# Second even attention of a two-block kernel on one core: heads in pairs on the two row halves of TensorE, values by half heads with a zero-padded V

## The chip, the cores and the metric

The kernel runs on one core of one Trainium2 chip. The metric is the device time of one execution in microseconds; given is the median of three runs. A core has TensorE (PE, matrix products into the PSUM banks), VectorE (DVE), ScalarE (ACT), GpSimd (POOL) and a DMA queue issued by SyncE (SP). The PSUM has 8 banks of 512 fp32 columns. TensorE's array has 128 rows; an operand that lies on 64 partitions uses one half of them.

## What is computed

Two blocks follow each other on 512 tokens of width 1024. The change lies in the even mixer of the second block, which runs two attentions side by side: a global one and one with a window of 128 tokens and a sink, each with 8 query heads and 2 key and value heads of width 64.

```python
def global_gqa(q, k, v):
...
        s = jnp.einsum('bqkgd,bskd->bkgqs', qi, k, preferred_element_type=jnp.float32) * scale
        p = jax.nn.softmax(s, axis=-1).astype(v.dtype)
        return jnp.einsum('bkgqs,bskd->bqkgd', p, v)

def windowed_gqa_sink(q, k, v, sink):
...
    valid = (jnp.abs(qpos - kpos) <= WINDOW) & (kpos >= 0) & (kpos < s_len)
    s = jnp.where(valid[None, :, None, None], s, NEG_INF)
    m = jnp.maximum(jnp.max(s, axis=-1), sk)
    p = jnp.exp(s - m[..., None])
    denom = jnp.sum(p, axis=-1) + jnp.exp(sk - m)
    p = (p / denom[..., None]).astype(v.dtype)
    o = jnp.einsum('bnkgqs,bnskd->bnqkgd', p, v_slab)

def even_mixer(h, w_in, q_gain, k_gain, sink, w_out, rope1, rope_axial):
    proj = h @ w_in
...
    oa = global_gqa(qa, ka, va)
...
    ob = windowed_gqa_sink(qb, kb, vb, sink)
    return jnp.concatenate([oa, ob], axis=-1) @ w_out
```

## The kernel before

Every fp32 matrix product is done as three products of rounded parts: each operand is split into a high part and the rest, and high x high, high x low and low x high are added in one bank (`PASSES`). The high part is written by ScalarE (a copy into fp32r), the low part by VectorE (a subtraction). Weights come through SP in groups of 128 x 1024, which POOL splits the same way (`split`, L296 to L300); most matmuls are in `group` (L384), a tile of 128 features by 512 tokens from one group. Each engine has one program with a fixed order of instructions, and semaphores between them; no scheduler moves anything.

The stage in question comes behind the projection `even2` (12 groups), whose last steps normalise and rotate queries and keys on VectorE and ScalarE, and ahead of the output projection `even2_out` (8 groups). Queries lie with features on partitions: tile i holds head i on partitions 0 to 63 and head 4 + i on partitions 64 to 127, and the keys and values of the two groups lie likewise. So a score product works on 64 rows, and its rows are those of the side s.

The work is cut into 64 units: u = 0 to 31 global, u = 32 to 63 banded; a unit is one head and one block j of 128 queries. `unit_b` orders them by group g, tile i, side s and block j, so four units of one head follow each other, then four of the other side. For one unit the steps are:

- `scores_b` (PE, L705): three matmuls of 64 rows, 512 columns in the global half, 256 or 384 (two or three chunks of keys) in the banded one, into one of three banks (4, 5, 0). It waits for the exp of unit u - 3.
- DVE takes the negated maximum (L1563); in the banded half it adds the mask, writes the sum to SBUF and takes the maximum in one instruction with a read-out behind it (L1571, twice), then brings in the sink (L1575).
- ACT takes the exp with a row sum (L1123), in the banded half also the exp of the sink (L1128); DVE the reciprocal (L1585, with L1583 ahead of it in the banded half); POOL scales the row (L338).
- `turn_b` (PE, L716): 2 to 4 transposes into bank 6 or 7, three units behind the scores.
- ACT copies the high part out (L1113), DVE subtracts for the low part (L1592), into `E_PT`.
- `values_b` (PE, L736): eight units behind the scores, when a head's four units are transposed. A step is one chunk of keys, three matmuls; four steps make a head, in bank 2 or 3 in turn. The stationary side is a chunk of `E_V` with 128 columns, those of both value heads, so both halves of the output fill and only that of the head's side is used. In the banded half the four steps have 512, 256, 384 and 256 columns; the first is whole so that it sets the bank, and for it POOL zeroes a corner of `E_PT` (L332).
- At the end of a head ACT copies the 64 partitions of its side (L1135) and DVE subtracts (L1599), into `Y2`.

PE goes through them as scores of u, values step of u - 8, transposes of u - 3:

```python
for u in range(64 + 8):
    if u == 3:
        pe.wait_ge(s_qlo, 22)
    if u < 64:
        scores_b(u)
    if u >= 8:
        values_b(u - 8)
    if 3 <= u < 67:
        turn_b(u - 3)
```

DVE's order for u is maximum of u, reciprocal of u - 1, low part of u - 3, and once in four units the output of a head. ACT's is high part of u - 3, exp of u, and the output of a head.

## Time and profile before

| | us |
|---|---|
| median of 3 runs | 2723.18 (2721.81 to 2744.44) |
| span of the profiled execution | 2728.4 |
| PE busy | 2627.8 (96%) |
| DVE busy | 1199.8 (44%) |
| ACT busy | 602.6 (22%) |
| POOL busy | 1572.9 (58%) |

No separate time of the profiled execution is given besides its span; the span lies 5.2 us above the median. Busy shares are sums over the whole program; matmuls are pipelined and their ends are modelled, so a busy PE may still be waiting in part. The granted clock of TensorE stands as a share of 2.4 GHz: 0.50 is 1.2 GHz. A duration of a row with "x3" goes from the start of the first to the modelled end of the last. In a chain each piece lasts until the next one takes over, so its pieces add up to the time. Times of rows are counted from the start of the span.

### The profile page before, as it was taken

The page shows a single profiled execution, that of the slowest core. Times are in us where ns is not written, and L with a number is a line of the kernel's source. Part 1 is how long each engine was busy: PE and PEld are TensorE (multiplying, and loading weights), DVE is VectorE, ACT ScalarE, POOL GpSimd, SP SyncE. Part 2 cuts the span into 40 slices and gives each one's busy share as a digit, 9 for nine tenths or more (in the row PEclk, how much of TensorE's full clock was granted, in tenths as well). Part 3 has the DMA queues.
Part 4 walks back from the last instruction along what each step waited for, and adds up shares of the span by engine and source line. Part 5 has one row for each costly group of instructions (what it writes and reads, how often), then busy time and mean ns, then how long its engine had stood idle before and what let it go on. Part 6 is the DMA issues. An engine that isn't in the chain of part 4 may idle for free.

```text
span 2728.4 us, 32300 instructions
## 1 busy us (share of the span) xinstructions
PE 2627.8 (96%) x11402; PEld 2046.6 (75%) x11402; DVE 1199.8 (44%) x1719; ACT 602.6 (22%) x1122; POOL 1572.9 (58%) x1329
## 2 busy tenths in 40 slices
PE   7999988999999999999999999999999998999998
PEld 2876446888788886667788887888887776788886
DVE  4353656446333314657533322333213777533311
ACT  3222431112111102256211111111102344211100
POOL 2523015666666775523666776676776664666675
PEclk9999999999999999889999999999999999999999
DMA  6311432333323332100332333333332211233332
GB/s 229 126 41 60 141 121 89 100 94 98 93 92 100 100 101 76 65 1 3 101 100 93 99 102 99 95 97 95 103 102 91 74 59 40 93 100 92 100 100 85
DMA packets 69058, 249.07 MB, mean 91 GB/s; under 512 B 7664, under 2 KB 10224, under 8 KB 68336
## 3 DMA queue, kind: packets, MB, share of 16 engines
q1 hardware_dynamic: 63936, 232.81, 27.3%
q10 hardware_dynamic: 5040, 15.16, 1.6%
q8 instruction: 51, 0.84, 0.1%
q14 instruction: 31, 0.25, 0.0%
HBM read 245.85 MB, written 2.10 MB: 91 GB/s over the span
## 4 chain that ended last, share of the span: by engine, by line
PE 89%; DVE 6%; ACT 2%; issue 2%; DMA 1%; POOL 0%; SPq 0%; ACTq 0%; DVEq 0%; POOLq 0%
PE pb L384 68%; PE pb L830 3%; PE pb L776 2%; PE pb L705 2%; PE pb L736 1%; PE pb L791 1%; PE pb L443 1%; PE pb L552 1%; PE pb L815 1%; PE pb L800 1%; PE pb L716 1%; PE pb L425 1%; PE pb L482 1%; PE pb L525 1%; PE pb L592 1%
## 5 line engine op out<-in xcount | busy, mean ns | idle before, releaser
L384 PE MATMUL pb<-ar,w_hi 128*128 128x512 f32 x5600 | 1739.2, 392 | 10.5 <-DVE ar L1264 4.5
L384 PEld LDWEIGHTS pb<-ar,w_hi 128*128 128x128 f32 x5600 | 1049.5, 188 | 246.5 <-issue 15.3
L384 PE MATMUL pb<-ar,w_lo 128*128 128x512 f32 x2800 | 1091.2, 390 | 0.0
L300 POOL TENSOR_TENSOR w_lo<-raw,w_hi 128x1024 fp32r<-128x1024 f32 x396 | 990.7, 2502 | 33.0
L296 POOL TENSOR_TENSOR still<-still 128x1 f32<-128x1 f32 x396 | 80.2, 202 | 932.0 <-PE pb L384 627.1
L384 PEld LDWEIGHTS pb<-ar,w_lo 128*128 128x128 f32 x2800 | 526.8, 188 | 110.4
L297 POOL TENSOR_SCALAR w_hi<-raw 128x1024 fp32r<-128x1024 f32 x396 | 421.0, 1063 | 0.0
L1522 DVE TENSOR_TENSOR tb<-pb,nb 128x512 f32<-128x512 f32 x88 | 60.9, 692 | 417.8 <-PE pb L384 417.8
L1443 DVE SCALAR_TENSOR_TENSOR x<-pb,x 128x512 f32<-128x512 f32 x48 | 36.5, 760 | 381.9 <-PE pb L384 381.9
L1528 DVE TENSOR_TENSOR ar<-tb,ar 128x512 f32 x88 | 156.2, 1775 | 91.0 <-ACT ar L1077 91.0
L1077 ACT ACTIVATE ar<-tb 128x512 f32 x88 | 55.7, 633 | 531.5 <-DVE tb L1525 531.5
L866 ACT ACTIVATE nb<-x 128x512 f32<-128x512 f32 x72 | 44.9, 625 | 382.9 <-DVE x L1443 377.2
L1075 ACT ACTIVATE tb<-tb 128x512 f32<-128x512 f32 x88 | 55.8, 634 | 252.1 <-DVE tb L1520 252.1
L1455 DVE SCALAR_TENSOR_TENSOR ar<-x,vec,ar 128x512 fp32r<-128x512 f32 x32 | 87.4, 2731 | 25.3 <-ACT ar L1038 25.3
L1520 DVE TENSOR_TENSOR tb<-pb,nb 128x512 f32<-128x512 f32 x88 | 60.9, 692 | 85.5 <-PE pb L384 85.5
L338 POOL TENSOR_SCALAR tb<-tb,tiny 128x512 f32<-128x512 f32 (+2 forms) x64 | 39.1, 612 | 102.9 <-DVE tiny L1585 102.9
L316 POOL TENSOR_TENSOR tb<-rt 128x256 f32<-128x256 f32 (+1 forms) x64 | 56.6, 887 | 67.9 <-PE pb L800 67.9
L1525 DVE TENSOR_TENSOR tb<-tb 128x512 f32<-128x512 f32 x88 | 87.9, 998 | 11.5
L830 PE MATMUL pb<-ar,w_hi 128*128 128x512 f32 x256 | 84.1, 409 | 0.0
L1222 DVE TENSOR_TENSOR nb<-nb 128x512 f32<-128x512 f32 (+1 forms) x70 | 73.3, 1047 | 21.1 <-ACT nb L866 19.6
L1038 ACT ACTIVATE ar<-x,vec 128x512 fp32r<-128x512 f32 x32 | 23.2, 724 | 210.8 <-DVE x L1443 210.8
L705 PE MATMUL pb<-ar 64*128 64x512 f32 (+2 forms) x192 | 63.2, 444 | 1.4 <-ACT tb L1123 1.4
(196 smaller groups left out, 2394.0 us busy)
## 6 DMA issues: line engine op xcount, KB each, us to landing
raw<-wstream SPq DMA_DIRECT2D x444, 512.0 KB, 3.5
x<-xt ACTq DMA_DIRECT2D x2, 2048.0 KB, 9.1
rt<-nbias ACTq DMA_DIRECT2D x16, 192.0 KB, 2.4
tb<-dft ACTq DMA_DIRECT2D x1, 2048.0 KB, 8.6
out<-x ACTq DMA_DIRECT2D x8, 256.0 KB, 2.2
tb<-ctxt ACTq DMA_DIRECT2D x1, 1024.0 KB, 13.4
rt<-rope ACTq DMA_DIRECT2D x1, 1024.0 KB, 4.8
rt<-nmask ACTq DMA_DIRECT2D x1, 640.0 KB, 3.8
```

Source lines behind the costliest of these rows:

```text
L296: pool.tensor_tensor(still[:, 0:1], still[:, 1:2], still[:, 2:3], ALU.add)
L297: pool.tensor_scalar(w_hi[:, n % SPLIT, :], raw[:, j, :], 1.0, 1.0, ALU.mult, ALU.mult)\
L300: pool.tensor_tensor(w_lo[:, n % SPLIT, :], raw[:, j, :], w_hi[:, n % SPLIT, :].bitcast(F32), ALU.subtract).then_inc(s_split, 1)
L384: mm = pe.matmul(pb[:, bank, :], W[a][:, n % SPLIT, k * P:(k + 1) * P], rhs(b, k0 + k), start=(first and k == 0 and i == 0), stop=(last an ...
L705: mm = pe.matmul(pb[:, S_BANKS[u % 3], 0:(hi - lo) * P], E_Q[g][a][rows, i, j * P:(j + 1) * P], E_K[g][b][rows, lo * P:hi * P], start=(q = ...
L830: mm = pe.matmul(pb[:, m % 2, :], W[a][:, m % SPLIT, k * P:(k + 1) * P], H[b][:, k, :], start=(k == 0 and i == 0), stop=(k == KT - 1 and i ...
L1222: dve.tensor_tensor(acc[:, 0:n], acc[:, 0:n], sq[k % 2][:, 0:n], ALU.add)\
L1455: dve.scalar_tensor_tensor(H[1][:, m, :], x[:, m, :], vcol(gain, i + m), H[0][:, m, :].bitcast(F32), ALU.mult, ALU.subtract)\
L1520: dve.tensor_tensor(tb[:, j, :], pb[:, 2 * j, :], rstd, ALU.mult).then_inc(s_ev, 1)
L1522: dve.tensor_tensor(tb[:, 4 + j, :], pb[:, 2 * j + 1, :], rstd, ALU.mult).then_inc(s_ev, 1)
L1525: dve.tensor_tensor(tb[:, 6 + j, :], tb[:, 2 + j, :], tb[:, 4 + j, :], ALU.mult)\
L1528: dve.tensor_tensor(tile(A_FFN[1], t * 2 + j), tb[:, 6 + j, :], tile(A_FFN[0], t * 2 + j).bitcast(F32), ALU.subtract)\
```

## The change

The 64 units become 32 pairs: w = 0 to 15 global, 16 to 31 banded. A pair is the two heads of one tile i (sides 0 and 1) for one block j.

- Scores: for each of the three passes one matmul on the rows of side 0 and one on those of side 1, into two banks: (0, 1) and (4, 5) in turn. They wait for both exps of pair w - 2.
- DVE takes the maxima of both banks in one instruction of 1024 columns in the global half; in the banded half two masked maxima and one tiny instruction for both sinks (whose negation is computed once ahead of the loop). The reciprocals of both heads are one instruction, now of pair w - 1 and ahead of the maxima of pair w.
- ACT takes two exps behind each other, in the banded half then two exps of sinks; POOL scales two rows.
- Transposes two pairs behind the scores, in three banks (3, 6, 7) in turn by head.
- Values four pairs behind the scores: one head of the pair, half of its queries (two blocks, 256 columns), all its chunks of keys, 12 matmuls of 256 columns in the global half; in the banded half 6 of 256 and 3 of 128 without the empty corners, so POOL's zeroing of corners of `E_PT` goes. The stationary side `E_VP` has 128 columns of which the 64 of the other side are zero, so both heads of a tile add into one bank, 2, for all tiles.
- Output: one copy and one subtraction of 128 partitions for two heads, once in four pairs; values of the next two heads wait for it.
- In `even2` POOL zeroes the four parts of `E_VP` (1024 columns each) between weight splits, and V is copied and subtracted in two pieces (64 columns of each chunk) where there was one.

The third attention keeps its own list of steps under a new name (`WHOLE`), and counts of semaphores that follow are adapted.

```diff
-        E_V = [[area(8192 + 6144 * g + 5120 + 512 * s, 4, P) for s in range(2)] for g in range(2)]
+        E_VP = [[ar[:, o:o + 8 * P].rearrange("p (s k c) -> p s k c", s=2, k=4)
+                 for o in (8192 + 6144 * g + 5120, 20480 + 1024 * g)] for g in range(2)]
...
-        S_BANKS = (4, 5, 0)
+        S_BANKS = ((0, 1), (4, 5))
+        T_BANKS = (3, 6, 7)
...
-        P_ROWS = (0, 1, 2, 4)
+        P_ROWS = ((0, 1), (2, 4), (5, 6))
...
+                if seg == "even2":
+                    for i in range(groups):
+                        split(g0 + i, n0 + i)
+                        if 2 <= i < 6:
+                            half = E_VP[(i - 2) // 2][i % 2]
+                            pool.memset(half.rearrange("p s k c -> p (s k c)").bitcast(F32), 0.0).then_inc(s_zero, 1)
+                    continue
...
-                    for u in range(64):
-                        if u in (34, 38):
-
-                            b = (u - 34) // 4
-                            pool.wait_ge(bt["o"], 7 + b)
-                            for part in range(2):
-                                pool.tensor_scalar(E_PT[b][part][:, 1, 3 * P:4 * P], ident, 0.0, 0.0, ALU.mult,
-                                                   ALU.mult).then_inc(s_zero, 1)
...
+                    for w in range(32):
+                        n = TOK if w < 16 else P * len(chunks_of(w % 4))
+                        pool.wait_ge(bt["r"], w + 1)
+                        for side in range(2):
+                            p = tb[:, P_ROWS[w % 3][side], 0:n]
+                            pool.tensor_scalar(p, p, tiny[:, 40 + 2 * (w % 4) + side:41 + 2 * (w % 4) + side], 1.0,
+                                               ALU.mult, ALU.mult).then_inc(bt["p"], 1)
...
+            def pair_b(w):
+
+                return w // 16, (w % 16) // 4, w % 4
+
+            def scores_b(w):
+                g, i, j = pair_b(w)
+                if w >= 2:
+                    pe.wait_ge(bt["e"], 2 * (w - 2) + 2)
                 lo, hi = (0, 4) if g == 0 else (chunks_of(j)[0], chunks_of(j)[-1] + 1)
                 for q, (a, b) in enumerate(PASSES):
-                    mm = pe.matmul(pb[:, S_BANKS[u % 3], 0:(hi - lo) * P], E_Q[g][a][rows, i, j * P:(j + 1) * P],
-                                   E_K[g][b][rows, lo * P:hi * P], start=(q == 0), stop=(q == 2))
-                mm.then_inc(bt["s"], 1)
...
-            def turn_b(u):
-                g, i, s, j = unit_b(u)
-                pe.wait_ge(bt["p"], u + 1)
-                if u >= 2:
-                    pe.wait_ge(bt["lo"], u - 1)
-                n = 4 if g == 0 else len(chunks_of(j))
...
-            GLOBAL = [(k, 0, 4) for k in range(4)]
-            BANDED = [(1, 0, 4), (0, 0, 2), (2, 1, 4), (3, 2, 4)]
...
-                if c == 0:
-                    pe.wait_ge(bt["lo"], 4 * head + 4)
-                    if head >= 2:
-                        pe.wait_ge(bt["ylo"], head - 1)
-                    if g == 1:
-                        pe.wait_ge(s_zero, 2 * (head % 2) + 2)
-                k, q0, q1 = (BANDED if g else GLOBAL)[c]
-                for q, (a, b) in enumerate(PASSES):
-                    mm = pe.matmul(pb[:, 2 + head % 2, q0 * P:q1 * P], E_V[g][a][:, k, :],
-                                   E_PT[head % 2][b][:, k, q0 * P:q1 * P],
-                                   start=(c == 0 and q == 0), stop=(c == 3 and q == 2))
-                if c == 3:
+                    for side in range(2):
+                        rows = slice(64 * side, 64 * side + 64)
+                        mm = pe.matmul(pb[:, S_BANKS[w % 2][side], 0:(hi - lo) * P],
+                                       E_Q[g][a][rows, i, j * P:(j + 1) * P], E_K[g][b][rows, lo * P:hi * P],
+                                       start=(q == 0), stop=(q == 2))
+                        if q == 2:
+                            mm.then_inc(bt["s"], 1)
+
+            def turn_b(w):
+                g, i, j = pair_b(w)
+                for side in range(2):
+                    n = 2 * w + side
+                    pe.wait_ge(bt["p"], n + 1)
+                    if n >= 3:
+                        pe.wait_ge(bt["lo"], n - 2)
+                    for c in range(4 if g == 0 else len(chunks_of(j))):
+                        mm = pe.transpose(pb[:, T_BANKS[n % 3], c * P:(c + 1) * P],
+                                          tb[:, P_ROWS[w % 3][side], c * P:(c + 1) * P], ident)
+                    mm.then_inc(bt["t"], 1)
+
+
+            GLOBAL = [[(k, 2 * half, 2 * half + 2) for k in range(4)] for half in range(2)]
+            BANDED = [[(1, 0, 2), (0, 0, 2), (2, 1, 2)], [(2, 2, 4), (3, 2, 4), (1, 2, 3)]]
+
+            def values_b(half, side):
+
+                head = half // 2
+                g = head // 4
+                pe.wait_ge(bt["lo"], 4 * half + 2 + side + 1)
+                if side == 0 and half % 2 == 0 and head >= 1:
+                    pe.wait_ge(bt["ylo"], head)
+                pieces = (BANDED if g else GLOBAL)[half % 2]
+                for c, (k, q0, q1) in enumerate(pieces):
+                    for q, (a, b) in enumerate(PASSES):
+                        mm = pe.matmul(pb[:, 2, q0 * P:q1 * P], E_VP[g][a][:, side, k, :],
+                                       E_PT[side][b][:, k, q0 * P:q1 * P],
+                                       start=(side == 0 and c == 0 and q == 0),
+                                       stop=(side == 1 and c == len(pieces) - 1 and q == 2))
+                if side == 1:
                     mm.then_inc(bt["o"], 1)
...
-            pe.wait_ge(s_vlo, 4)
+            pe.wait_ge(s_vlo, 6)
...
+            for w in range(32 + 4):
+                if w == 1:
                     pe.wait_ge(s_qlo, 22)
-                if u < 64:
-                    scores_b(u)
-                if u >= 8:
-                    values_b(u - 8)
-                if 3 <= u < 67:
-                    turn_b(u - 3)
+                if w < 32:
+                    scores_b(w)
+                if 2 <= w < 34:
+                    turn_b(w - 2)
+                if w >= 4:
+                    values_b((w - 4) // 2, w % 2)
...
+                    for side in range(2):
+                        cols = slice(64 * side, 64 * side + 64)
+                        act.activation(E_VP[m - 8][0][:, side, :, cols],
+                                       pb[:, m - 4, :].rearrange("p (k c) -> p k c", k=4)[:, :, cols], ACT.Copy)\
+                            .then_inc(s_vhi, 1)
...
+                if w >= 8 and w % 4 == 0:
+                    head = (w - 8) // 4
+                    act.wait_ge(bt["o"], 2 * head + 2)
+                    act.activation(Y2[0][:, head, :], pb[:, 2, :], ACT.Copy).then_inc(bt["yhi"], 1)
...
+                    act.wait_ge(bt["mx"], w + 1)
+                    if w >= 3:
+                        act.wait_ge(bt["t"], 2 * (w - 3) + 2)
+                    for side in range(2):
+                        p, col = tb[:, P_ROWS[w % 3][side], 0:n], 2 * (w % 4) + side
+                        act.activation(p, pb[:, S_BANKS[w % 2][side], 0:n] if g == 0 else p, ACT.Exp,
+                                       bias=tiny[:, 8 + col:9 + col], accum_out=tiny[:, 16 + col:17 + col])\
+                            .then_inc(bt["e"], 1)
...
+                    v = w - 1
+                    c = 2 * (v % 4)
+                    dve.wait_ge(bt["e"], 2 * v + 2)
+                    total = tiny[:, 16 + c:18 + c]
+                    if v >= 16:
+                        dve.wait_ge(bt["es"], 2 * (v - 16) + 2)
+                        b = 36 + 2 * (v % 2)
+                        link(dve.tensor_tensor(tiny[:, b:b + 2], total, tiny[:, 24 + c:26 + c], ALU.add))
+                        total = tiny[:, b:b + 2]
+                    dve.reciprocal(tiny[:, 40 + c:42 + c], total).then_inc(bt["r"], 1)
+                if w < 32:
...
-                        dve.tensor_reduce(mx, pb[:, S_BANKS[u % 3], :], AX.X, ALU.max, negate=True)\
+                        dve.tensor_reduce(tiny[:, 8 + c:10 + c], pb[:, s0:s1 + 1, :], AX.X, ALU.max, negate=True)\
...
+                        dve.wait_ge(bt["t"], 2 * (w - 3) + 2)
+                        b = 32 + 2 * (w % 2)
+                        for side in range(2):
+                            link(dve.tensor_tensor_reduce(tb[:, P_ROWS[w % 3][side], 0:n],
+                                                          pb[:, S_BANKS[w % 2][side], 0:n], wm[:, first:first + n],
+                                                          1.0, -3.0e38, ALU.add, ALU.max,
+                                                          tiny[:, b + side:b + side + 1]))
+                        dve.scalar_tensor_tensor(tiny[:, 8 + c:10 + c], tiny[:, b:b + 2], -1.0, minus_sink[:, :, i],
+                                                 ALU.mult, ALU.min).then_inc(bt["mx"], 1)
+                if w >= 8 and w % 4 == 0:
+                    head = (w - 8) // 4
                     dve.wait_ge(bt["yhi"], head + 1)
-                    dve.tensor_tensor(Y2[1][rows, 4 * g + i, :], pb[rows, 2 + head % 2, :],
-                                      Y2[0][rows, 4 * g + i, :].bitcast(F32), ALU.subtract)\
-                        .then_inc(bt["ylo"], 1)
+                    dve.tensor_tensor(Y2[1][:, head, :], pb[:, 2, :], Y2[0][:, head, :].bitcast(F32),
+                                      ALU.subtract).then_inc(bt["ylo"], 1)
```

TensorE in the global half, where the first values come in (names: `pb` the PSUM, `ar` queries, values and probabilities in SBUF, `mat,tb` identity and probability rows; the size is that of the output). Before:

```order
L705 MATMUL pb<-ar 128x512 x3
L716 MATMUL pb<-mat,tb 128x128 x4
L705 MATMUL pb<-ar 128x512 x3
L736 MATMUL pb<-ar 128x512 x3
L716 MATMUL pb<-mat,tb 128x128 x4
L705 MATMUL pb<-ar 128x512 x3
```

After, where L708 are scores, L722 transposes and L740 values:

```order
L708 MATMUL pb<-ar 128x512 x6
L722 MATMUL pb<-mat,tb 128x128 x8
L708 MATMUL pb<-ar 128x512 x6
L722 MATMUL pb<-mat,tb 128x128 x8
L740 MATMUL pb<-ar 128x256 x12
L708 MATMUL pb<-ar 128x512 x6
```

Before, one unit is 3 scores, 3 values and 4 transposes; after, a pair is 6 scores, 8 transposes and 12 values of half the width, in this order.

TensorE in the banded half, before, for the four units in which the first banded head's values are computed:

```order
L705 MATMUL pb<-ar 128x256 x3
L736 MATMUL pb<-ar 128x512 x3
L716 MATMUL pb<-mat,tb 128x128 x3
L705 MATMUL pb<-ar 128x384 x3
L736 MATMUL pb<-ar 128x256 x3
L716 MATMUL pb<-mat,tb 128x128 x3
L705 MATMUL pb<-ar 128x384 x3
L736 MATMUL pb<-ar 128x384 x3
L716 MATMUL pb<-mat,tb 128x128 x2
L705 MATMUL pb<-ar 128x256 x3
L736 MATMUL pb<-ar 128x256 x3
```

And after:

```order
L708 MATMUL pb<-ar 128x256 x6
L722 MATMUL pb<-mat,tb 128x128 x6
L740 MATMUL pb<-ar 128x256 x6
L740 MATMUL pb<-ar 128x128 x3
L708 MATMUL pb<-ar 128x384 x6
L722 MATMUL pb<-mat,tb 128x128 x4
L740 MATMUL pb<-ar 128x256 x6
L740 MATMUL pb<-ar 128x128 x3
```

The values of a head went from four steps of 512, 256, 384 and 256 columns, one per unit, to two parts of 256, 256 and 128 columns, one per pair.

VectorE in the banded half. Before, in one unit (L1571 masked maximum and its read-out, L1575 sink, L1583 and L1585 sum and reciprocal of the unit before, L1592 low part, L1599 output of a head):

```order
L1571 ISA tb,tiny<-pb,tb 128x256
L1571 ISA tiny 128x1
L1575 TENSOR_SCALAR tiny<-tiny,vec 128x1
L1583 TENSOR_TENSOR tiny<-tiny 128x1
L1585 RECIPROCAL tiny<-tiny 128x1
L1592 TENSOR_TENSOR ar<-pb,ar 128x2x128
L1599 TENSOR_TENSOR ar<-pb,ar 64x512
L1571 ISA tb,tiny<-pb,tb 128x256
```

After (L1583 and L1585 sum and reciprocals of the pair before, L1601 masked maxima, L1605 sinks, L1610 output, L1620 low parts):

```order
L1583 TENSOR_TENSOR tiny<-tiny 128x2
L1585 RECIPROCAL tiny<-tiny 128x2
L1601 ISA tb,tiny<-pb,tb 128x256
L1601 ISA tiny 128x1
L1601 ISA tb,tiny<-pb,tb 128x256
L1601 ISA tiny 128x1
L1605 SCALAR_TENSOR_TENSOR tiny<-tiny 128x2
L1610 TENSOR_TENSOR ar<-pb,ar 128x512
L1620 TENSOR_TENSOR ar<-pb,ar 128x3x128 x2
```

The reciprocal moved from behind the maximum of the next unit to ahead of the maxima of the next pair, and the output stands between maxima and low parts.

## Rows read from the trace of the kernel before

**Rows 1.** Cores: span and mean granted clock.

```profile
core 0: 2728.4 us, clock 0.977
```

**Rows 2.** Stretches: length, then busy by engine, granted clock, DMA share, GB/s.

```profile
1137.10:1184.90 47.80, 46.44 (x117) 28.81 (x117) 22.93 (x46) 18.44 (x44) 10.04 (x15) 0.50 0.05 15
1184.90:1221.90 37.00, 37.00 (x168) 24.39 (x167) 25.34 (x55) 22.88 (x53) 11.07 (x16) 1.00 0.01 1
1221.90:1277.00 55.10, 54.05 (x278) 38.61 (x276) 45.33 (x193) 42.02 (x133) 17.86 (x35) 1.00 0.00 1
...
1044.90:1055.10 10.20, 6.50 (x13) 3.29 (x13) 7.05 (x11) 4.57 (x8) 1.87 (x1) 0.50 0.18 61
```

**Rows 3.** Chain that ended last, end of the stage: start, us, what.

```profile
1284.89 5.22 PE pb L384 x23
```

**Rows 4.** Chain, global half at half clock.

```profile
1159.62 1.58 PE pb L705 x3
...
1162.78 0.85 PE pb L716 x4
```

**Rows 5.** Chain, global half at full clock.

```profile
1215.34 0.89 PE pb L705 x3
...
1217.12 0.44 PE pb L716 x4
```

**Rows 6.** Instructions in order of time, PE, first attention (L568, L569 its scores).

```profile
289.44 0.50 PE L568 MATMUL pb<-ar 64*128 64x512 f32 x1
...
289.89 0.51 PE L568 MATMUL pb<-ar 64*128 64x512 f32 x2
...
291.16 0.60 PE L443 MATMUL pb<-raw,c_win 128*8 128x512 f32 x1
```

**Rows 7.** Instructions in order of time, PE, values of both widths.

```profile
1216.15 0.96 PE L736 MATMUL pb<-ar 128*128 128x512 f32 x3
...
1269.14 0.62 PE L736 MATMUL pb<-ar 128*128 128x256 f32 x3
```

**Rows 8.** Groups of the stage by shape: busy, mean ns, idle before, releaser.

```profile
L338 POOL TENSOR_SCALAR tb<-tb,tiny 128x512 f32<-128x512 f32 x32 | 22.1, 692 | 66.6 <-DVE tiny L1585 66.6
L1592 DVE TENSOR_TENSOR ar<-pb,ar 128x512 fp32r<-128x512 f32 x32 | 22.0, 688 | 30.0 <-ACT ar L1113 30.0
L1123 ACT ACTIVATE tb<-pb,tiny 128x512 f32<-128x512 f32 x32 | 21.8, 683 | 3.1 <-DVE tiny L1563 3.0
L1563 DVE TENSOR_REDUCE tiny<-pb 128x1 f32<-128x512 f32 x32 | 21.8, 684 | 3.7 <-PE pb L705 3.5
L1113 ACT ACTIVATE ar<-pb 128x512 fp32r<-128x512 f32 x32 | 19.1, 597 | 38.3 <-PE pb L716 38.3
```

**Rows 9.** Groups by shape, first attention (262 to 382 us).

```profile
L1392 DVE TENSOR_REDUCE tiny<-pb 128x1 f32<-128x768 f32 x30 | 27.2, 950 | 0.0
```

**Rows 10.** Groups by shape, banded half (1221.9 to 1277 us).

```profile
L1123 ACT ACTIVATE tb<-tb,tiny 128x384 f32<-128x384 f32 x16 | 9.8, 615 | 3.7 <-DVE tiny L1575 3.5
L1571 DVE CUSTOM_DVE_ANT_0 tb<-pb,tb 128x384 f32<-128x384 f32 x16 | 8.8, 548 | 0.0
L1128 ACT ACTIVATE tiny<-tiny,vec 128x1 f32<-128x1 f32 x30 | 8.4, 280 | 0.0
L1123 ACT ACTIVATE tb<-tb,tiny 128x256 f32<-128x256 f32 x15 | 7.6, 509 | 7.2 <-DVE tiny L1575 7.2
L1571 DVE CUSTOM_DVE_ANT_0 tb<-pb,tb 128x256 f32<-128x256 f32 x15 | 6.2, 415 | 0.1
```

**Rows 11.** Instructions in order of time, start of the stage.

```profile
1136.98 4.14 PE L705 MATMUL pb<-ar 64*128 64x512 f32 x9
...
1140.84 1.28 DVE L1563 TENSOR_REDUCE tiny<-pb 128x1 f32<-128x512 f32 x2
```

**Rows 12.** Groups by shape, POOL, 1040 to 1137 us.

```profile
L300 POOL TENSOR_TENSOR w_lo<-raw,w_hi 128x1024 fp32r<-128x1024 f32 x14 | 36.0, 2568 | 1.2
L297 POOL TENSOR_SCALAR w_hi<-raw 128x1024 fp32r<-128x1024 f32 x13 | 16.1, 1237 | 0.0
```

145 lines of the change are left out of this document (50 added, 95 removed).

## The prediction

> **What bounds the kernel now.** I read the mean clock of the core first, then a table of stretches, then the chain that ended last, and last the single instructions. The execution spans 2728.4 us at a mean granted clock of 0.977 [rows 1]. The changed stage, the second block's even attention, begins with its first scores at 1137.0 and gives way to the projection behind it at 1284.7, where a chain piece of 23 plain 512-column products begins: 5.22 us, so 0.227 us each [rows 2, 3]. The first is the start of its first matmul [rows 11]; the unit with which the banded half begins starts at 1221.9. That is 147.7 us for 64 units (32 global, 32 banded). The table shows three regimes. From 1137.1 to 1184.9 TensorE is busy 46.4 of 47.8 us, at half its clock (1.2 GHz). From 1184.9 to 1221.9 it is busy all the time at 2.4 GHz. In the banded half (1221.9 to 1277.0) it still reads 54.05 of 55.10, but those ends are modelled; VectorE at 45.3 and ScalarE at 42.0 are close behind.
>
> In the global half the chain consists of TensorE alone: 3 scores, 3 values, 4 transposes. A unit takes 1.58 + 1.58 + 0.85 = 4.01 us at 1.2 GHz [rows 4] and 0.89 + 0.89 + 0.44 = 2.22 us at 2.4 GHz [rows 5]; values last as long as scores in both. Three 512-column products are worth 3 x 0.227 = 0.68 us; the 0.2 us more of each group is what going between 64-row and 128-row work costs (last results out, first weights uncovered). So each unit pays for two such turns.
>
> **What the change makes of a global pair on TensorE.** Before, a pair of units costs 2 x 2.22 = 4.44 us at full clock and 8.02 at half.
> - Scores: still six matmuls, but every other one on the other 64 rows and into another bank. That two row halves run side by side is seen in the first attention of this very trace, where the second half is issued behind the first: 12 matmuls (six of 512, six of 256 columns) lie between 289.44 and 291.16, 1.72 us, and two of one shape start within one row [rows 6]. One after another they would take 6 x 0.227 + 6 x 0.12 = 2.08 and one turn of 0.2, 2.3 in all; only part of the first half's stream was left when the second began, so 1.72 is no limit. I take full overlap: six for the time of three, 0.89 (1.58 at half clock). The other bound is no overlap: 1.57 (2.86).
> - Transposes: the same 8, and one approach instead of two: 0.96 (1.75).
> - Values: 12 of 256 columns for 6 of 512. The zero-padded V takes no columns away; it lets both heads add into one bank. Three values of 256 columns last 0.62 us to their modelled end, three of 512 last 0.96 [rows 7]; of this 0.34, 0.11 is the shorter last one, so each step falls from 0.23 to about 0.12. 12 x 0.12 + 0.1 for the first weights = 1.54 (2.73 at half).
> - Sum: 3.39 us a pair at full clock and 6.1 at half, against 4.44 and 8.02.
>
> **Is the other side fast enough?** VectorE now takes the reciprocal of pair w-1 before the maxima of pair w, so exp is wholly in a ring: maxima, two exps, reciprocal, maxima. A 1024-column maximum isn't in the trace. 512 columns take 0.684 [rows 8] and 768 take 0.950 [rows 9]; I take 1.21 by that slope, at most 1.37 for two of 512. Exp is 0.68 each [rows 8], 1.6 for two with their sums. With 0.2 for the reciprocal and handovers the ring is 3.0, under 3.39. ScalarE's two copies (0.60 each) fit beside the maxima and VectorE's two subtractions (0.69 each) beside the exps [rows 8]. POOL's two scalings (1.4) have a pair's time of room.
>
> What is late next is the single output bank. Before, heads alternate between banks 2 and 3; now bank 2 must be copied (0.60) and subtracted (0.69) before the next two heads' values may start. VectorE has the maxima of the same turn ahead of it: scores ready at 0.96 after the turn begins, maxima 1.12 until the next may start, subtraction 0.69, so about 2.85, while TensorE, through scores and transposes, would start values at 1.75. Stall: 1.1 us once in 4 pairs.
>
> **Banded pairs.** TensorE's own work falls to about 2.4 us a pair, since 12 values of 352 columns on average become 9 of 213. The ring sets the pace. With 384 columns: 0.30 (sink sum, reciprocal) + 2 x 0.59 (masked maximum 0.548 and its read-out) + 0.25 + 2 x 0.615 (exp) + 0.47 (two sink exps, 0.28 each, overlapped) = 3.43; with 256 columns 0.415 and 0.509 stand in place of these, and the sum is 2.98 [rows 10]. Mean 3.2. The bank-2 wait, here behind 256-column maxima, delays scores of the next pair by about 0.8 every fourth pair: 3.4 us. Before it is 55.1/16 = 3.44 [rows 2]. I expect nothing here. Bounds: 2.6 (TensorE alone) to 4.1 (the ring and then two 0.45 copies behind it).
>
> **The clock.** Between 1137.1 and 1184.9 the granted clock is half [rows 2]. The low stretch behind ffn0, 1044.9 to 1055.1, ended after 10.2 us with plain 128-row products; this one lasted 47.8 us with half its matmuls on 64 rows one at a time and four turns for two units. After the change both halves of the array work at once in the scores and half the turns go, so work per time at 1.2 GHz rises by 8.02/6.1. I take it that the clock is back once values are running, about 1157.5 (estimate); the other bound is 1184.9, as before. Each us at half clock costs 1 - 3.66/6.1 = 0.4 us.
>
> **Sum, in this execution's time.** VectorE is free of the key and query chain at 1140.84 [rows 11]. Sink negation 0.3, maxima 1.21, exps 1.6: 1143.8 (pair 0's scores are ready before). Then TensorE is the chain at half clock: three times scores (1.58) and transposes (1.75) and one values (2.7), 12.7: pair 5 begins at 1156.5. Before, unit 10 begins one unit behind 1159.62, at 1163.6 [rows 4]. Pair 5, half in either clock, ends at 1160.4. Pairs 6 to 15: 10 x 3.39 + 2 stalls x 1.1 = 36.1, to 1196.5; before 1221.9. Banded: 16 x 3.4 = 54.4, to 1250.9. Tail: scaling, transposes, copy and subtraction of the last pair, then two values of 1.05: 5.7, to 1256.6; before 1284.7. Gain 28.1 us.
>
> Outside the stage: V is split in two 256-column pieces per group instead of one of 512, on VectorE, which is the late engine there: +0.2 each, 0.4. Four POOL memsets of 1024 columns go between weight splits; the nearest row, a 1024-column POOL pass, is 1.24 us [rows 12]. A group is 24 x 0.227 = 5.45 us of TensorE and a split is that pass and one of 2.57, 3.8 in all, so 3.8 + 1.24 = 5.0 stays hidden; uncovered it would be 4 x 1.24 = 5.0. Taken at 0. SP's queue and all DMAs are untouched. Net -27.7: 2728.4 becomes 2700.7. The span lies 5.2 above the median of the runs, 2723.2, to which I carry the same difference: 2695.5, said as 2696.
>
> **Rivals.**
> 1. The clock returns only at 1184.9. For: mixes of transposes and matmuls kept it low for 47.8 us before. Against: the denser work. Time: 27.4 x 0.4 = 11 less gain, 2707. The Trainium skill, "TensorE: Matmul & The Clock Gate", Part 4, says transposes don't count as busy for the gate; their share of a pair's time rises here from 0.88/4.44 to 0.96/3.39, which speaks for this rival. No run here shows that rule by itself.
> 2. The evacuation takes the lead: copies don't fit beside the maxima, and a global pair takes 3.0 + 1.2 = 4.2, or a banded pair half a us more than now. For: ScalarE and VectorE already wait for each other there. Against: in the global half the chain never leaves TensorE. 10 x 0.8 less the 2.2 of stalls that this would swallow, or 16 x 0.5: 6 to 8 less, 2703. The skill's "TensorEngine Tiling (Array Packing)", PSUM Bottleneck, warns of just this: tiling speeds the array and not the emptying of PSUM.
> 3. The change doesn't do what it says: the halves don't overlap in turns. 0.68 x 10 + 1.28 x 5 = 13 less: 2709.
> 4. Slower: thinner work on TensorE keeps the clock at 1.2 GHz through the whole stage. Global pairs 6.1 each to the end (1156.5 + 11 x 6.1 = 1223.6), banded about 4.1 x 16 (the 2.4 us with the columns' part doubled), tail 8: 1297, 12 us later than now: 2736. It decides from a return later than about 1228. Against: 37 us at 2.4 GHz with turns twice as frequent did not lower it.
>
> **Chances.** Forecast 0.55 (own range 2690 to 2701), rival 1 0.15, rival 2 0.15, rival 3 0.07, rival 4 0.03, and 0.05 for more than I count (the clock back sooner, banded pairs at 3.0: 2686). Range 2687 to 2712. One per cent of the median, 27.2 us, is about what a measurement of this kernel can tell; it lies at 2696.0, on my forecast: faster by over 1% 0.45 (half the forecast's share and the upper tail, and some of the rivals' lower edges), within 1% 0.51, slower 0.04.
>
> **What would show it.** Scores of the two sides starting nearly together, six in about 0.9 us; global pairs 3.4 us apart with one longer by 1.1 in four, TensorE waiting there for VectorE's output subtraction; clock at 1.0 from about 1157; banded pairs at 3.2 to 3.4, with ScalarE and VectorE waiting for each other; the projection starting at 1256. Wrong if scores of a pair take 1.5 us, if the low clock lasts past 1170, or if banded pairs need over 3.8.

## The result, and the profile after

Seven runs of the changed kernel have a median of 2712.7 us (2702.8 to 2712.8), seven of the kernel before beside them 2728.7 us: a ratio of 0.9927, with a 95% interval of 0.9900 to 0.9953 (it is formed from all the executions; the quotient of the two medians, 0.9942, lies inside the interval). Measured twice more it was 0.9935 (0.9911 to 0.9960) and 0.9918 (0.9888 to 0.9948). The change makes the kernel faster by 16 to 19 us, 0.6 to 0.8%, which is within 1%. The prediction had said 2696, with a range of 2687 to 2712.

The mean clock of the profiled execution, against [rows 1]:

```profile
core 0: 2701.0 us, clock 0.981
```

The stage, in stretches cut where the granted clock steps (start and end in us, then busy us and instructions of each engine; PEclk is the granted clock as a share of 2.4 GHz), against [rows 2]:

```profile
1136.50:1146.80 10.30, 7.10 (x27) 4.04 (x26) 6.42 (x10) 3.94 (x10) 2.31 (x4) 0.51 0.24 70
1146.80:1197.10 50.30, 46.30 (x354) 37.76 (x352) 40.56 (x68) 37.77 (x95) 20.42 (x31) 1.00 0.00 1
1197.10:1211.60 14.50, 11.79 (x96) 10.10 (x97) 10.31 (x37) 9.88 (x33) 4.16 (x9) 1.00 0.00 1
1211.60:1215.00 3.40, 3.40 (x19) 2.96 (x17) 1.96 (x7) 1.84 (x5) 0.78 (x2) 0.51 0.02 5
...
1225.30:1228.70 3.40, 3.40 (x18) 2.85 (x18) 1.50 (x7) 0.57 (x3) 0.93 (x2) 0.51 0.00 0
1238.90:1245.80 6.90, 6.24 (x30) 5.60 (x30) 3.72 (x12) 3.54 (x13) 0.93 (x2) 0.51 0.00 1
```

Two things are to be seen. The long stretch at 1.2 GHz at the start, 47.8 us in [rows 2], is 10.3 us long. And the banded half, which ran wholly at 2.4 GHz before, now has three short stretches at 1.2 GHz, 13.7 us in all.

TensorE in the global half, pair by pair (start, us, engine, line; L708 are scores, L722 transposes, L740 values; in brackets how long it stood idle and for what), against [rows 5]:

```profile
1159.92 0.96 PE L708 MATMUL pb<-ar 64*128 64x512 f32 x6
1160.82 1.09 PE L722 MATMUL pb<-mat,tb 128*128 128x128 f32 x8
1161.66 1.67 PE L740 MATMUL pb<-ar 128*128 128x256 f32 x12
1163.26 0.96 PE L708 MATMUL pb<-ar 64*128 64x512 f32 x6
1164.15 1.09 PE L722 MATMUL pb<-mat,tb 128*128 128x128 f32 x8
1166.26 0.95 PE L740 MATMUL pb<-ar 128*128 128x256 f32 x6 [1.01 <-DVE ar L1610]
...
1192.47 0.62 PE L708 MATMUL pb<-ar 64*128 64x256 f32 x6
```

A pair takes 1163.26 - 1159.92 = 3.34 us, and six scores on two row halves 0.96. Every fourth pair TensorE waits for VectorE's subtraction of the output (L1610), because there is one output bank. The banded half begins at 1192.47 (before: 1221.9), the projection at 1258.85 (before: 1284.7):

```profile
1258.85 0.67 PE L386 MATMUL pb<-ar,w_hi 128*128 128x512 f32 x2
```

So the global half and its start gained 29.4 us, and the banded half with its tail gave 3.6 of them back: 66.4 us in place of 62.8. Two groups of the stage, the maximum over two banks and the masked maximum, against [rows 8 to 10]:

```profile
L1591 DVE TENSOR_REDUCE tiny<-pb 128x2 f32<-128x1024 f32 x16 | 19.5, 1217 | 3.7 <-PE pb L708 3.4
L1601 DVE CUSTOM_DVE_ANT_0 tb<-pb,tb 128x256 f32<-128x256 f32 (+1 forms) x32 | 15.7, 491 | 6.9 <-PE pb L708 6.3
```

The waits of the banded half (us in total, times, longest), from 1197 to 1259:

```profile
DVE tiny L1583 <- ACT tiny L1147: 11.5, 12, 1.2
PE pb L740 <- DVE ar L1610: 9.6, 4, 2.6
ACT tb L1141 <- DVE tiny L1605: 7.4, 11, 1.0
DVE tb L1601 <- PE pb L708: 6.3, 4, 2.3
```

Read as a circle: the sum (L1583) waits for the sink exponentials (L1147), the exponentials (L1141) for the maxima (L1605), and the maxima stand behind the sum on VectorE. VectorE and ScalarE take turns instead of working side by side. Four times TensorE stands still for 1.7 to 2.6 us at the output bank. One of these standstills, and the products behind it:

```profile
1221.42 0.52 PE L722 MATMUL pb<-mat,tb 128*128 128x128 f32 x3 [0.51 <-DVE ar L1620]
...
1223.73 0.68 DVE L1610 TENSOR_TENSOR ar<-pb,ar 128x512 fp32r<-128x512 f32 x1
...
1224.56 1.63 PE L740 MATMUL pb<-ar 128*128 128x256 f32 x9 [2.63 <-DVE ar L1610]
...
1226.12 1.33 PE L708 MATMUL pb<-ar 64*128 64x384 f32 x6
```

The clock falls at 1225.3, and six scores of 384 columns last 1.33 us there instead of 0.79. The same is to be seen at the start of the stage already in the trace of the kernel before. There TensorE stood 2.54 us for VectorE just ahead of the stage, and the low stretch of [rows 2] begins at 1137.1:

```profile
1135.92 1.13 PE L507 MATMUL pb<-tb,mat 128*128 128x512 f32 x2 [2.54 <-DVE tb L1328]
```

### The profile page after: what moved, and what is told of

It reads as the page before. It is cut to its first block, busy times and chain, and to the rows that moved or that the text cites. A ratio compares the mean times of both kernels' runs of the same rounds, so it can differ in the third digit from the quotient of the medians.

```text
span 2701.0 us, 32413 instructions
## 1 busy us (share of the span) xinstructions
PE 2584.8 (96%) x11546; PEld 2032.9 (75%) x11546; DVE 1183.5 (44%) x1634; ACT 595.4 (22%) x1116; POOL 1574.8 (58%) x1329
## 4 chain that ended last, share of the span: by engine, by line
PE 89%; DVE 6%; ACT 2%; issue 2%; DMA 1%; POOL 0%; SPq 0%; DVEq 0%; ACTq 0%; POOLq 0%
PE pb L386 69%; PE pb L837 3%; PE pb L781 2%; PE pb L445 2%; PE pb L796 1%; PE pb L554 1%; PE pb L740 1%; PE pb L822 1%; PE pb L805 1%; PE pb L427 1%; PE pb L484 1%; PE pb L527 1%; DVE ar L1279 1%; PE pb L594 1%; ACT tb L1141 1%
## 5 line engine op out<-in xcount | busy, mean ns | idle before, releaser
L386 PE MATMUL pb<-ar,w_hi 128*128 128x512 f32 x5600 | 1736.7, 391 | 11.5 <-DVE ar L1276 4.8
L1537 DVE TENSOR_TENSOR tb<-tb 128x512 f32<-128x512 f32 x88 | 87.6, 995 | 11.5
L445 PE MATMUL pb<-raw,c_win 128*8 128x512 f32 x128 | 61.4, 605 | 0.6 <-DVE ar L1378 0.6
```

The costliest lines, as they stand in the source:

```text
L386: mm = pe.matmul(pb[:, bank, :], W[a][:, n % SPLIT, k * P:(k + 1) * P], rhs(b, k0 + k), start=(first and k == 0 and i == 0), stop=(last an ...
L445: mm = pe.matmul(pb[0:8, 0, :], c_win[:, k, 7 - q:15 - q], raw[:, g % RAW, kk * TOK:(kk + 1) * TOK], start=(i == 0 and kk == 0), stop=(i = ...
L1537: dve.tensor_tensor(tb[:, 6 + j, :], tb[:, 2 + j, :], tb[:, 4 + j, :], ALU.mult)\
```

## The experiments

All are edits of the changed kernel or of one another, with 4 to 12 executions each (and one more of the kernel before). "Stage" is the time from the first scores to the projection in the profiled execution, read from rows such as those above; before the change it is 147.7 us and in the changed kernel 121.7. Three theories stood at the outset: the gain is the overlap of the row halves and what it does to the clock; the gain is the merged work of VectorE and ScalarE; what was given back in the banded half is the output bank's wait, the clock's falls, or the evacuation ring.

| run | median us | ratio to before (95%) | stage us |
|---|---|---|---|
| again | 2708.2 | 0.9935 (0.9911 to 0.9960) | 124.7 |
| again_2 | 2705.5 | 0.9918 (0.9888 to 0.9948) | 125.2 |
| apart | 2711.0 | 0.9932 (0.9904 to 0.9960) | 125.0 |
| one_half | 2728.8 | 0.9997 (0.9978 to 1.0016) | 144.4 |
| low_first | 2703.7 | 0.9915 (0.9888 to 0.9942) | 119.0 |
| two_banks | 2696.5 | 0.9891 (0.9864 to 0.9918) | 113.2 |
| fill | 2703.8 | 0.9911 (0.9877 to 0.9944) | 119.8 |
| late_recip | 2696.3 | 0.9869 (0.9838 to 0.9900) | 110.5 |
| two_banks_late | 2686.8 | 0.9833 (0.9803 to 0.9863) | 102.5 |
| best_one_half | 2705.5 | 0.9926 (0.9908 to 0.9944) | 121.6 |

**The changed kernel again.** No edit.

> The changed kernel once more, unaltered. The profiled execution had the clock at 1.2 GHz for 10.3 us at the stage's start and 13.6 us in three stretches of the banded half, and was about 10 us below the median of the others. Theory (the clock's short falls in the banded half and where it returns at the start vary from one execution to the next): 2703 to 2713 us, and if the profiled execution is near 2713, its extra time stands at half clock inside this stage. Rival (the difference comes from other stages): the stage from the first scores (1137.1 us) to the projection (1259.0 us) keeps its 121.9 us within 1 us and another stage is longer.

Its stage is 3.0 us longer than in the first profiled execution, with four falls of the clock in the banded half instead of three:

```profile
1210.10:1216.90 6.80, 5.58 (x26) 5.06 (x27) 4.25 (x15) 3.12 (x12) 1.37 (x3) 0.52 0.01 2
...
1227.10:1230.60 3.50, 3.50 (x20) 2.95 (x19) 1.54 (x7) 0.64 (x5) 0.93 (x2) 0.54 0.00 0
...
1240.80:1247.60 6.80, 5.68 (x27) 5.16 (x27) 4.15 (x15) 3.12 (x12) 1.27 (x3) 0.52 0.00 1
...
1257.90:1261.30 3.40, 3.40 (x20) 3.40 (x18) 0.76 (x2) 0.66 (x2) 0.00 (x0) 0.53 0.03 5
```

20.5 us at 1.2 GHz instead of 13.7. This execution is 5.4 us longer than the first profiled one (2708.2 against 2702.8), and 3.0 of these lie in the stage. So part of the spread between runs of the changed kernel lies here; the rest of it, and of the 10 us between the first profiled execution and its own median, stays open.

**Order of the scores.** The six matmuls by sides instead of in turns:

```
-                for q, (a, b) in enumerate(PASSES):
-                    for side in range(2):
+                for side in range(2):
+                    for q, (a, b) in enumerate(PASSES):
```

> The six score matmuls of a pair in the order of sides (three of side 0, then three of side 1) instead of in turns. Theory (in turns the two row halves run beside each other, 0.89 us for six at 2.4 GHz in this stage before): six take some 1.3 to 1.5 us, 0.4 to 0.6 us more in each of 16 global pairs where PE sets the pair: 6 to 10 us more in all. Rival (the hardware overlaps neighbours of different row halves as well where only one such pair of neighbours stands, or the evacuation ring hides it): within 2 us.

The theory's number was wrong. (The 0.89 us that the expectation calls six scores are three in the kernel before, [rows 5]; six in turns take 0.96.) By sides, six scores still take 0.97 us and a pair 3.35:

```profile
1173.12 0.97 PE L708 MATMUL pb<-ar 64*128 64x512 f32 x6
1174.02 1.09 PE L722 MATMUL pb<-mat,tb 128*128 128x128 f32 x8
1174.87 1.67 PE L740 MATMUL pb<-ar 128*128 128x256 f32 x12
1176.47 0.74 PE L708 MATMUL pb<-ar 64*128 64x512 f32 x4
```

The median is 2.8 us above its neighbour's, with intervals that overlap. Writing the matmuls in turns is not what buys the overlap.

**No second row half.** Both sides read rows 0 to 63, so side 1's output is another one:

```
-                        rows = slice(64 * side, 64 * side + 64)
+                        rows = slice(0, 64)
```

> Both heads' scores read rows 0 to 63 (side 1 gets side 0's operands, so its output is not the reference's); nothing else is changed, and no two score matmuls stand on different row halves. Theory (the two row halves run beside each other, whatever the order of the six, which is why the order of sides made no difference): six take about 1.5 to 1.6 us instead of 0.95 at 2.4 GHz, PE's pair grows by some 0.6 us in each of 16 global pairs, less in the banded half: 8 to 14 us slower than the changed kernel. Rival (the gain of the overlap is hidden behind DVE's and ACT's ring of about 3.0 us a pair): under 4 us.

It costs 20.6 us against the changed kernel's 2708.2, more than expected, and the kernel then stands level with the one before the change (what else it carries is told apart below). TensorE at 2.4 GHz:

```profile
1167.69 1.65 PE L708 MATMUL pb<-ar 64*128 64x512 f32 x6
1169.27 1.09 PE L722 MATMUL pb<-mat,tb 128*128 128x128 f32 x8
1170.12 1.67 PE L740 MATMUL pb<-ar 128*128 128x256 f32 x12
1171.72 0.50 PE L708 MATMUL pb<-ar 64*128 64x512 f32 x1
```

Six scores 1.65 instead of 0.96, a pair 4.03 instead of 3.34: 0.69 us each, the three 512-column products of [rows 3] (0.68). The clock too comes back later, after 23.9 us instead of 6.8 to 13.7:

```profile
1135.50:1159.40 23.90, 23.09 (x68) 16.41 (x66) 14.71 (x21) 11.13 (x27) 6.45 (x9) 0.50 0.11 31
```

**The output's low part first.** VectorE's subtraction of the output is put ahead of the pair's maxima:

```
+                if w >= 8 and w % 4 == 0:
+                    head = (w - 8) // 4
+                    dve.wait_ge(bt["yhi"], head + 1)
+                    dve.tensor_tensor(Y2[1][:, head, :], pb[:, 2, :], Y2[0][:, head, :].bitcast(F32),
+                                      ALU.subtract).then_inc(bt["ylo"], 1)
                 if w < 32:
...
-                if w >= 8 and w % 4 == 0:
-                    head = (w - 8) // 4
-                    dve.wait_ge(bt["yhi"], head + 1)
-                    dve.tensor_tensor(Y2[1][:, head, :], pb[:, 2, :], Y2[0][:, head, :].bitcast(F32),
-                                      ALU.subtract).then_inc(bt["ylo"], 1)
```

> DVE takes the output's low part ahead of the pair's maxima instead of behind them. Theory (PE's wait is as long as two maxima of 0.56 us and the small operation behind them, some 1.2 us, that stand ahead of the low part): the banded wait falls from 2.6 to about 1.4 us and the global from 1.25 to about 0; maxima each fourth pair are some 0.6 us later, so 2 to 8 us less in all, and the clock falls less often. Rival (maxima are on the ring that sets the pair, and ACT's copy of the output is what ends late): within 2 us of the changed kernel, DVE waiting for ACT at the low part.

4.5 us less than its neighbour, as the theory had it. TensorE's wait at the output bank over the whole stage, the changed kernel (again) and then this one:

```profile
PE pb L740 <- DVE ar L1610: 13.1, 7, 2.6
```

```profile
PE pb L740 <- DVE ar L1589: 7.2, 5, 1.7
```

The clock still falls four times in the banded half, so that part of the expectation failed. None of TensorE's waits there is longer than 1.72 us now, so a fall does not take one of 2.6 us. One of the four waits, and a stretch behind another:

```profile
1238.17 1.24 PE L740 MATMUL pb<-ar 128*128 128x256 f32 x9 [1.72 <-DVE ar L1589]
```

```profile
1223.00:1229.00 6.00, 5.44 (x25) 4.92 (x26) 4.49 (x17) 3.23 (x12) 1.63 (x4) 0.50 0.00 0
```

**Two output banks.** Heads alternate between banks 2 and 3, and the transposes keep two banks instead of three:

```
-        T_BANKS = (3, 6, 7)
+        T_BANKS = (6, 7)
...
-                    if n >= 3:
-                        pe.wait_ge(bt["lo"], n - 2)
+                    if n >= 2:
+                        pe.wait_ge(bt["lo"], n - 1)
...
-                if side == 0 and half % 2 == 0 and head >= 1:
-                    pe.wait_ge(bt["ylo"], head)
+                if side == 0 and half % 2 == 0 and head >= 2:
+                    pe.wait_ge(bt["ylo"], head - 1)
```

> Output alternates between banks 2 and 3 head by head, transposes keep banks 6 and 7; PE no longer waits each fourth pair for the low part of the last output. Theory (that wait costs 1.25 us four times in the global half and 2.6 us three or four times in the banded half, and the clock falls to 1.2 GHz after it in the banded half): no PE wait on the output's low part, no stretch at 1.2 GHz after 1197, projection starts about 8 to 14 us before 1259.0, time 8 to 14 us below the changed kernel. Rival A (evacuation by DVE and ACT sets the banded pair, the output wait only shows where their delay lands): less than 4 us below. Rival B (two transpose banks instead of three make a new wait of PE on the low parts at each pair): not below, the wait stands at the transposes line.

11.7 us less than the changed kernel beside it: the theory's range. The clock stays at 2.4 GHz. What is left in the banded half are the waits of the circle and, as rival B said, one at the transposes; since the same two transpose banks leave almost no wait once the circle is cut (two_banks_late), it is mostly the circle that shows there (both from 1197 to 1252; first the clock from 1150):

```profile
1150.00:1252.00 102.00, 89.21 (x709) 74.76 (x707) 78.79 (x210) 75.06 (x221) 35.88 (x61) 1.00 0.01 1
```

```profile
ACT tb L1141 <- DVE tiny L1605: 12.5, 15, 1.3
PE pb L722 <- DVE ar L1620: 11.8, 11, 1.7
DVE tiny L1583 <- ACT tiny L1147: 11.4, 12, 1.2
```

**The clock by itself.** Twenty matmuls of 256 columns that nobody reads stand ahead of each of the four banded output waits; the waits stay:

```
+                if side == 0 and half in (8, 10, 12, 14):
+                    w = 2 * half + 4
+                    pe.wait_ge(bt["lo"], 2 * w - 4)
+                    for i in range(20):
+                        pe.matmul(pb[:, T_BANKS[(2 * w - 2) % 3], 0:2 * P], E_VP[g][0][:, 0, 0, :],
+                                  E_VP[g][0][:, 0, 0:2, :].rearrange("p k c -> p (k c)"), start=True, stop=True)
```

> In the banded half only, ahead of each of TensorE's four waits for the output's low part, 20 matmuls of 256 columns are put whose result nobody reads (into the transposes' bank that is free then); the wait itself stays. They take about 2.2 us of the wait of 2.6 us. Theory (the stretches at 1.2 GHz in the banded half are the result of TensorE standing still there, and cost time of their own beside the wait): the clock stays at 2.4 GHz from the global half to the projection, and the kernel is 4 to 10 us faster than the unaltered changed kernel, though work is added and no wait is removed. Rival A (the clock's fall costs nothing, since DVE and ACT set the pair): within 2 us. Rival B (the matmuls run into the time when the bank is free and delay the pair): slower by up to 4 us.

> The changed kernel unaltered, beside the filled one on the same chip: 2706 to 2713 us by either theory; stretches at 1.2 GHz in the banded half of 14 to 24 us in all.

The banded half in the filled kernel, and then in the unaltered one beside it:

```profile
1197.00:1259.00 62.00, 57.04 (x455) 49.70 (x454) 40.71 (x147) 38.26 (x131) 16.64 (x32) 1.00 0.01 2
```

```profile
1197.00:1259.00 62.00, 48.29 (x327) 41.45 (x327) 37.17 (x137) 36.06 (x124) 15.69 (x30) 0.83 0.00 1
```

Mean clock 1.00 against 0.83: the falls come from TensorE's standstill, and useless work in it prevents them. The stage is 5.4 us shorter than beside it (119.8 against 125.2), and 1.9 to 5.4 us shorter than in the four profiled executions with falls and a single output bank (121.7, 124.7, 125.2, and apart's 125.0). In the medians only 1.7 us are seen, 2703.8 (2702.0 to 2705.0) against 2705.5 (2699.8 to 2708.0), which is less than the expectation and not told apart from nothing. So the mechanism is shown, and its worth only within the stage of profiled executions.

**The reciprocals behind the maxima.** Undoes one part of the change: on VectorE the sum and reciprocal of pair w-1 stand behind the maxima of pair w again, in the order that the kernel before had.

```
 for w in range(32 + 5):
-    if 1 <= w < 33:
-        ...
-        dve.reciprocal(tiny[:, 40 + c:42 + c], total).then_inc(bt["r"], 1)
     if w < 32:
         ...
+    if 1 <= w < 33:
+        ...
+        dve.reciprocal(tiny[:, 40 + c:42 + c], total).then_inc(bt["r"], 1)
     if w >= 8 and w % 4 == 0:
```

> Undoes one part: the reciprocals of the pair before stand behind the pair's maxima on DVE again, as before the change, instead of ahead of them. Theory (in the banded half maxima, exponentials, sink exponentials, sum and reciprocal follow one another in one ring of about 3.0 to 3.4 us; behind the maxima the ring is cut, since the next maxima no longer wait for ACT): the maxima stop waiting behind DVE's wait for the sink exponentials (11.4 us before), but POOL's scaling and the transposes come later; with the single output bank still in place the banded half falls by 2 to 6 us. Rival (the placement ahead of the maxima is what feeds PE; the transposes then wait for POOL and the pair grows): 3 to 8 us slower than the changed kernel, PE waiting at the transposes for POOL.

11.9 us below the changed kernel (both against kernels before of 2727.1), double the most that was expected. The single output bank is still there, yet its longest wait is 1.4 us and no fall of the clock is left in the stage (the wait in the banded half, and the clock from 1149):

```profile
PE pb L740 <- DVE ar L1610: 5.1, 4, 1.4
```

```profile
1149.00:1246.60 97.60, 89.03 (x699) 74.23 (x698) 73.17 (x207) 72.53 (x217) 35.90 (x60) 1.00 0.01 1
```

The sum's wait for the sink exponentials, 11.5 us before, is down to 0.7, since VectorE does the maxima meanwhile. The output wait shrank as well, likely because VectorE is no longer late when the output is ready; that wasn't tried by itself.

**Both together.**

> The same on top of two output banks (which took 2696.5 us and had no stretch at 1.2 GHz behind 1157). Theory: with PE busy only some 4.8 us in 6 of the banded half there the DVE and ACT ring sets the pair, 3.35 us; cut, a pair costs DVE's own work (two maxima 1.3, small operation and reciprocal 0.5, two low parts 1.0) 2.9 us, so 5 to 7 us less: about 2690. Rival (PE sets it at the transposes through POOL): 2697 to 2702.

2686.8 us, 9.7 below two banks alone: more than expected. Behind the cut ring TensorE itself sets the pair, at 2.6 us, and VectorE's work fits into less than the 2.9 us that the expectation gave it.

```profile
1147.80:1240.30 92.50, 90.60 (x712) 75.19 (x711) 75.36 (x210) 75.04 (x223) 36.97 (x62) 1.00 0.01 2
```

TensorE is busy 90.6 of 92.5 us. This version beats both kernels: 0.9833 of the one before, 21.4 us below the changed one.

**No second row half in the best version.** The edit of "one_half" once more, on this one.

> Two output banks and the late reciprocals, with both heads' scores on rows 0 to 63 (side 1's output is not the reference's). The same edit cost the changed kernel 20.6 us. Theory (0.69 us in each of 16 global pairs is 11 us, a shorter term in the banded half, and the clock's later return at the start): with no wait for the output bank left to hide in, the banded pairs are TensorE's own too, 0.4 to 0.5 us each, and it costs 18 to 28 us: about 2705 to 2715. Rival (most of the 20.6 us was the clock falling more often in the banded half): under 14 us, below 2701.

18.7 us more, inside the range. The two were not measured side by side: each against the kernel before beside it, they gain 40.3 and 20.6 us, 19.7 apart. Where the loss lies can be added up from the starts of pairs' scores. The first five pairs lose 7.03 us, most of it (by estimate) to the clock, which is back after 23.8 us instead of 10.3; the next eleven, all global, lose 7.54, 0.69 each; and the banded pairs some 0.3 each, 4.33. That makes 18.9 of the 19.1 by which the stage is longer.

```profile
1136.70:1160.50 23.80, 22.97 (x67) 16.10 (x66) 14.45 (x20) 11.11 (x27) 6.62 (x9) 0.51 0.09 31
1160.50:1259.00 98.50, 97.83 (x671) 84.31 (x671) 69.72 (x200) 68.51 (x206) 32.96 (x56) 1.00 0.01 1
```

**The kernel before again.**

> The kernel before, once more with a profile. Theory (without the overlap and with fewer columns per microsecond in the stage's first pairs the 1.2 GHz stretch at the start is long): it lasts some 40 to 50 us again from near 1137. Rival (its 47.8 us were an accident of one execution): under 25 us, and the execution's time then is 10 us or more below 2728.

```profile
1137.90:1182.30 44.40, 43.59 (x108) 26.64 (x109) 22.08 (x43) 16.73 (x40) 10.45 (x14) 0.50 0.06 17
```

44.4 us at 1.2 GHz, in the one execution taken, of 2728.5 us: the long low stretch of [rows 2] was no accident.

## Why the prediction was right or wrong

Faster, but by less than 1%, was in its chances (0.51 for within 1%) and the first median fell on the range's upper end (2712.7, with 2708.2 and 2705.5 later). The forecast itself, 2696, was 10 to 17 us too low; as a gain it was 27.7 us, and 16 to 19 came. By its own steps:

1. **A global pair of 3.39 us: right.** Measured 3.34, with scores 0.96 for 0.89, and 4.03 when the halves can't overlap. The reason given, two row halves at once, holds. The detail that the text tied to it, "every other one on the other 64 rows" in turns, is not needed: by sides they overlap as well. The Trainium skill's "TensorEngine Tiling (Array Packing)", Key Properties, says that different tiles can load weights and multiply in parallel and asks for no order; the 0.97 us of the run by sides agree. That 0.2 us of each group is the cost of going between 64-row and 128-row work, as the sum had it, no run tried by itself.
2. **Evacuation in the global half: right.** The 1024-column maximum took 1.217 us (taken: 1.21), and the chain stays on TensorE. The stall of 1.1 us once in four pairs measured 4.59 - 3.34 = 1.25 (1167.85 - 1163.26 is the long pair).
3. **The clock's return: too late.** Forecast 1157.5, measured 1146.8, and in the other profiled executions with overlap 1145.8 to 1150.5. Pair 5 began at 1153.2 instead of 1156.5 and the banded half at 1192.5 instead of 1196.5. Rival 1 (1184.9) is wrong. The forecast took it that the values had to be running first; the clock was back before the first of them (1151.6). The experiments say what shortened the stretch from 44 to 48 us: without overlap, but with the rest of the change, it is 24 us, with it 7 to 14. So the rest of the change takes 20 to 24 us off it and the overlap 10 to 17; which of the other edits does it wasn't separated. (A slip of 0.15 stands in this sum, 1140.84 + 0.3 + 1.21 + 1.6 being 1143.95; and the 1160.4 follows from a clock back at 1157.5, not from a pair run half in either clock. Neither matters here.)
4. **"I expect nothing here", the banded half: the step that failed.** 60.1 us were forecast from the first banded scores to the projection and 66.4 came, 6.3 us more (9 to 10 in the executions with four falls). By the starts of scores, in us:

| | forecast | changed | with filling (no falls) | two banks (no falls) |
|---|---|---|---|---|
| banded pairs 1 to 5 | 17.0 | 18.8 | 18.8 | 15.2 |
| pairs 6 to 13 | 27.2 | 30.3 | 28.0 | 26.4 |
| from pair 14 to the projection | 15.9 | 17.2 | 17.3 | 17.8 |
| together | 60.1 | 66.4 | 64.0 | 59.4 |

Two terms are wrong. The first is the clock, which the prediction left out of this half: it counted TensorE's standstill as time alone and never as something that lowers the clock behind it. Beside the filled kernel the falls cost 2.3 us here, in pairs 6 to 13 (30.3, 30.6 and 31.1 us in the three executions of the unaltered kernel, against 28.0), and 5.0 and 6.4 us over the half in the two of them with four falls. The filling may delay a little itself, so these are lower bounds. The second is the price of the output wait. In pairs 6 to 13 it is 28.0 - 26.4, 0.8 per four pairs, just what was forecast. But in pairs 1 to 5, where no fall comes before 1211.6, its first two occurrences cost 1.7 and 2.2 us (pairs of 4.67 and 5.49 against 2.99 and 3.28 with two banks). The circle itself, 3.30 a pair with two banks, was sized nearly right at 3.2 (its smaller term adds up to 2.95 and not 2.98). From pair 14 on the forecast is 1.3 to 1.9 us short in all three; why wasn't tried.

Two of the rows behind the second line, scores of the sixth and of the fourteenth banded pair, in the kernel with two banks and then in the changed one:

```profile
1207.75 0.79 PE L708 MATMUL pb<-ar 64*128 64x384 f32 x6
...
1234.17 0.79 PE L708 MATMUL pb<-ar 64*128 64x384 f32 x6
```

```profile
1211.31 1.15 PE L708 MATMUL pb<-ar 64*128 64x384 f32 x6
...
1241.64 1.33 PE L708 MATMUL pb<-ar 64*128 64x384 f32 x6
```

5. **The argument against rival 4 failed with it.** "37 us at 2.4 GHz with turns twice as frequent did not lower it" is true of a TensorE that is always busy, as it was there; it says nothing of one that stands still for 2.6 us. It says nothing, either, of TensorE's wait of 2.54 us ahead of the stage, behind which the long low stretch of the same trace begins. The rival itself (low through the whole stage for thinner work) did not come, but a low clock did, in pieces, and from standing still: thin work without a wait kept 2.4 GHz (two_banks_late).
6. **The ring was priced and not seen as a loss.** The prediction worked out 3.43 and 2.98 for it, found the mean equal to the 3.44 of before, and stopped. That equality hid two opposite parts: TensorE's work in a banded pair had become much shorter, and the ring that the moved reciprocals made kept all of it. With the old order of two operations and two banks a banded pair takes 2.58 us (20.65 us for the same eight pairs), and moving them cost 9.7 us in the whole kernel with two banks and 11.9 with one. The bound that the text gave for this, 2.6 by TensorE alone, is where the pair then stands.
7. **Outside the stage: nothing speaks against it.** The first scores start at 1137.14 (before 1136.98 [rows 11]). But this start lies anywhere from 1134.5 to 1139.3 in the thirteen profiled executions, so whether V's split and the four fills cost the 0.4 us taken, or nothing, can't be read from it. The 5.0 us that uncovered fills would cost aren't seen: the start is 1137.4 on average of the eleven with the change and 1138.2 of the two without.
8. **Carrying the difference to the median.** In the profiled executions the forecast is near by chance: -27.7 forecast, 2728.4 - 2701.0 = 27.4 measured, but 4.0 us were gained on it before the banded half, 6.3 lost in that half and 1.5 gained behind the stage, and the execution was at the fast end of its own runs. The medians say 16 to 19.
9. **Rival 3 was priced too low.** No overlap was put at 13 us; it costs 19 to 21, since the clock comes back later and the banded pairs pay as well.

The whole change can now be written as a sum of medians. Pairs instead of units, without overlap, with two output banks and the reciprocals behind the maxima (best_one_half beside its kernel before): 2726.1 to 2705.5, -20.6 us. In the profiled executions 17.3 us of the stage's gain lie ahead of the banded scores and 8.8 behind, where the values also have fewer columns (352 by 12 before, 213 by 9 now). The overlap of the row halves: to 2686.8, -18.7. The reciprocals ahead of the maxima: to 2696.5, +9.7. One output bank: to 2708.2, +11.7. That is -17.9. It had to come out near the 18.9 measured directly, since each step ends on the median where the next begins; it shows how the gain divides in this order and is no second proof of it. So two of the three theories hold side by side, the overlap and the pairing (fewer turns of TensorE, fewer columns in the banded values, merged work beside it and an earlier clock, not told apart), and more than half of what they bring was spent again on two details. The forecast saw the last of these too small and without its effect on the clock, and the one before it not at all. Medians of the kernel before spread over several us, so the first term is the least sure.

## What to carry to other kernels

Two equal groups of matmuls on different row halves ran in nearly the time of one (0.96 us for six, where six on one half took 1.65), in whichever order they were written, but what that buys can go to the next ring. Look which operations on the evacuating engines wait for each other, and don't put the use of another engine's last result ahead of work that could run meanwhile. A wait of TensorE costs more than its length when the clock falls behind it: here waits of 1.7 to 2.6 us were followed, nearly every time, by 3.4 to 6.9 us at half speed. Where a forecast says that a stage stays the same because two unlike limits come out equal, move one of them in an experiment first.
